# Two decoder layers on one core: the compress of the cached pages moved behind the projection, the first feed-forward's output product in three passes

## The reference

```python
def _layer(x, f_in, f_out, g, b, mixer):
    x = _ln(ALPHA * x + 0.5 * _swiglu(x, f_in[0], f_out[0]), g[0], b[0])
    m, new = mixer(x)
    x = _ln(ALPHA * x + m, g[1], b[1])
    x = _ln(ALPHA * x + 0.5 * _swiglu(x, f_in[1], f_out[1]), g[2], b[2])
    return x, new

def _swiglu(x, w_in, w_out):
    gate, up = jnp.split(x @ w_in, 2, axis=-1)
    return (jax.nn.silu(gate) * up) @ w_out

def _compress(x, pe, w1, w2):
    B, L, K, D = x.shape
    sub = x.reshape(B, L // CMP_STRIDE, CMP_STRIDE, K, D)
    first = jnp.einsum('bnjkd,jde->bnke', sub, w1[:CMP_STRIDE])
    second = jnp.einsum('bnjkd,jde->bnke', sub, w1[CMP_STRIDE:])
    pe_term = jnp.einsum('jd,jde->e', pe, w1)
    hid = jax.nn.gelu(first[:, :-1] + second[:, 1:] + pe_term)
    return jnp.einsum('bnke,ed->bnkd', hid, w2)
```

## Time and profile before

| what | value |
|---|---|
| timed runs, median of 3 | 2906.67 us (2905.1 to 2910.49) |
| the profiled execution | 2892.05 us, its span 2890.5 us |
| TensorE busy / DVE / ACT / POOL | 92% / 36% / 26% / 12% of the span |
| mean granted clock of TensorE | 0.938 |
| bytes moved | 265.81 MB, mean 92 GB/s |
| chain that ended last | PE 49%, issue 37%, DVE 4%, POOL 3%, DMA 2% |

### The profile page before, as it was taken

One profiled execution on the slowest core, in us unless ns is written; L12 is line 12 of the kernel. 1 busy time (PEld: TensorE's weight loads), 2 busy tenths in 40 slices (PEclk: granted clock), 3 DMA queues, 4 the chain that ended last, 5 costly groups with the idle time before them and its releaser, 6 DMA issues.

```text
span 2890.5 us, 49314 instructions
## 1 busy us (share of the span) xinstructions
PE 2668.9 (92%) x17788; PEld 2379.9 (82%) x17788; DVE 1046.9 (36%) x2036; ACT 764.2 (26%) x1167; POOL 342.8 (12%) x321
## 2 busy tenths in 40 slices
PE   7999999997789899999899999999978998999996
PEld 7999788896356889999889997888944567999995
DVE  2222121535555642232432211224456557222415
ACT  2222000422243332231232210013213433222313
POOL 0000000024231200013100000001241311000240
PEclk9999999997699899999999999999955999999998
DMA  3222443114431122222122234321153301222222
GB/s 134 88 87 87 156 137 111 53 61 138 138 86 45 59 69 88 87 88 81 70 88 87 87 105 155 126 91 61 46 179 103 89 30 59 88 87 87 89 80 80
DMA packets 110003, 265.81 MB, mean 92 GB/s; under 512 B 15348, under 2 KB 85139, under 8 KB 90771
## 3 DMA queue, kind: packets, MB, share of 16 engines
q1 hardware_dynamic: 99778, 233.21, 23.9%
q0 software_dynamic: 10080, 30.73, 3.3%
HBM read 258.15 MB, written 14.24 MB: 94 GB/s over the span
## 4 chain that ended last, share of the span: by engine, by line
PE 49%; issue 37%; DVE 4%; POOL 3%; DMA 2%; SPq 2%; DVEq 1%; ACT 1%; POOLq 1%; PEldq 0%; PEld 0%; ACTq 0%
PE PS L458 48%; POOL wo_lo L389 2%; SPq L315 1%; POOL wi_lo L447 1%; DVEq L1424 1%; DMA WO<-wo_dram 1%; POOLq L398 1%; DMA M<-slc_k_dram 1%; DVE xs L1542 0%; DMA WI<-wi_dram 0%; POOLq L402 0%; DVE sm L1888 0%; DVE wi_lo L1427 0%; DVE Z L1719 0%; DVE Z L1427 0%
## 5 line engine op out<-in xcount | busy, mean ns | idle before, releaser
L458 PE MATMUL PS<-xs,wi_hi 128*128 128x272 f32 x5376 | 1018.7, 289 | 20.3 <-DVE wi_lo L1427 18.4
L458 PE MATMUL PS<-xs,wi_lo 128*128 128x272 f32 x3088 | 898.9, 291 | 0.0
L458 PEld LDWEIGHTS PS<-xs,wi_hi 128*128 128x128 f32 x5376 | 849.0, 190 | 21.6 <-issue 21.6
L458 PEld LDWEIGHTS PS<-xs,wi_lo 128*128 128x128 f32 x3088 | 589.7, 191 | 0.0
L389 POOL TENSOR_TENSOR wo_lo<-WO,wo_hi 128x2816 fp32r<-128x2816 f32 x24 | 151.0, 6291 | 1911.6 <-ACT wo_hi L1113 1911.6
L458 PE MATMUL PS<-H,WO 128*128 128x272 f32 x1408 | 332.1, 397 | 6.3 <-DMA WO<-wo_dram 4.8
L1427 DVE TENSOR_TENSOR wi_lo<-WI,wi_hi 128x2048 fp32r<-128x2048 f32 x85 | 194.8, 2292 | 368.7 <-ACT wi_hi L1113 368.7
L458 PEld LDWEIGHTS PS<-H,WO 128*128 128x128 f32 x1408 | 269.0, 192 | 67.3 <-issue 12.0
L458 PE MATMUL PS<-wo_hi,xs 128*128 128x352 f32 x960 | 239.2, 328 | 14.6 <-DVE xs L1542 8.2
L1113 ACT ACTIVATE wi_hi<-WI 128x2048 fp32r<-128x2048 f32 x85 | 162.7, 1914 | 289.1 <-DMA WI<-wi_dram 289.1
L458 PE MATMUL PS<-h_hi,wo_hi 128*128 128x272 f32 x704 | 207.2, 294 | 24.5 <-POOL wo_lo L389 14.1
(11 more groups left out here) (202 smaller groups left out, 3095.4 us busy)
## 6 DMA issues: line engine op xcount, KB each, us to landing
WI<-wi_dram SPq DMA_DIRECT2D x100, 1024.0 KB, 4.8
WO<-wo_dram SPq DMA_DIRECT2D x44, 1408.0 KB, 6.0
M<-cmp_t_dram SPq DMA_DIRECT2D x256, 128.0 KB, 2.2
M<-slc_k_dram SPq DMA_DIRECT2D x128, 64.0 KB, 2.1
M<-slc_k_dram POOLq DMA_DIRECT2D x128, 64.0 KB, 2.5
M<-slc_v_dram SPq DMA_DIRECT2D x128, 64.0 KB, 2.1
M<-slc_v_dram POOLq DMA_DIRECT2D x128, 64.0 KB, 2.3
o_win_s_dram<-win_rows_dram POOLq DMA_DIRECT2D x2, 4064.0 KB, 4.0
```

Source lines behind the costliest of these rows:

```text
L458: return nc.tensor.matmul(out, lhsT, rhs, start=start, stop=stop, skip_group_check=True)
```

## The change

The first feed-forward's output product now runs the same code as the second's (`ffn_out(l, f)`), with `round_h`, `low_h`, `low_wo` and `squares` called for it too. h_hi then takes the regions of the compressed keys, so the whole compress moves behind the projection, into a new `compress(l)` on TensorE, ACT and DVE, where it is interleaved with `rows_to_cols` and the prompt's compressed attention. SP and POOL load 8 of a member's 16 pages each. The half of a hidden sum that lies on partitions 0 to 63 is copied by ACT and added by DVE in one operation. `slc_scores(0)` moves from ahead of the attention to unit 4, and every later piece of the table AT by 4 or more units. The two DRAM copies move from behind the first slc_k pages on POOL's queue to right behind the load of PR at the start of the layer. On DVE the gate weights are masked before the rope, and the gMLP's normalisation stands in member 4's turn of the compress.

```diff
@@ -41,11 +41,11 @@
-AT = dict(keys_1=0, cmp_scores=1, cmp_softmax=2, cmp_weights=4, cmp_turn=5, cmp_columns=6, cmp_outputs=7, cmp_take=8,
...
+AT = dict(keys_0=4, keys_1=8, cmp_scores=1, cmp_softmax=2, cmp_weights=4, cmp_turn=5, cmp_columns=6, cmp_outputs=7, cmp_take=8,
...
-CR_DMAS = 4 * NPG + 1 + 2 * NPG + 2 * NPG
+CR_DMAS = 2 * NPG + 1 + 2 * NPG + 2 * NPG
+CR_LATE = 6 * NPG
+NWS = 2 * KD + NCH - 2
...
@@ -294,16 +306,14 @@
-            def load_pages(l, first, n, src, p, width):
-
-                with sp.Fori(0, n // LOT) as g:
-                    pages = nc.values_load_multi_w_load_instructions(
-                        pt_sb[0:1, ds(first + LOT * g, LOT)], engines=[mybir.EngineType.SP],
-                        min_val=0, max_val=NPHYS - 1)[1]
-                    for j, page in enumerate(pages):
-                        sp.dma_start(CR[:, p, ds((LOT * g + j) * width, width)],
-                                     src[ds(l * NPHYS + page, 1), :, :].rearrange("o p n -> p (o n)")
-                                     ).then_inc(cr_full[p], 16)
+            def load_batch(l, b, p):
+
+                pages = nc.values_load_multi_w_load_instructions(
+                    pt_sb[0:1, ds(b * NPG, LOT)], engines=[mybir.EngineType.SP], min_val=0, max_val=NPHYS - 1)[1]
+                for j, page in enumerate(pages):
+                    sp.dma_start(CR[:, p, j * 256:(j + 1) * 256],
+                                 cmp_t[ds(l * NPHYS + page, 1), :, :].rearrange("o p n -> p (o n)")
+                                 ).then_inc(cr_full[p], 16)
...
@@ -334,19 +344,19 @@
-                with sp.Fori(0, B // 2) as i:
-                    for p in range(2):
-                        b = 2 * i + p
-                        load_wo(l, b, p)
-                        sp.wait_ge(cr_freed, at(l, NCR, b + 1))
-                        own(sp)
-                        load_pages(l, b * NPG, NPG, cmp_t, p, 256)
+                ffn_out(l, 0)
                 with sp.Fori(0, NCH // 2) as i:
                     for p in range(2):
                         load_wo(l, KD + 2 * i + p, p)
 
                 sp.wait_ge(wo_done, at(l, NWO, KD + NCH + 2))
                 own(sp)
+                with sp.Fori(0, B // 2) as i:
+                    for p in range(2):
+                        sp.wait_ge(cr_freed, at(l, NCR, 2 * i + p + 1))
+                        own(sp)
+                        load_batch(l, 2 * i + p, p)
+
                 def load_groups(first, src):
                     with sp.Fori(0, 2) as a:
...
@@ -389,6 +399,26 @@
+            def copies(l):
+
+                lw = lw_of(l)
+                ops = lw(o_pool_s, "o b s n -> (o b) s n")
+                pool.dma_start(ops[:, 0:11, :], lw(hist_rows, "o b s n -> (o b) s n")[:, 4:15, :]).then_inc(stored, 16)
+                ows = lw(o_win_s, "o b s n -> (o b) s n")
+                pool.dma_start(ows[:, 0:508, :], lw(win_rows, "o b s n -> (o b) s n")[:, 4:512, :]).then_inc(stored, 16)
+
+            def load_batch(l, b, p):
+
+                pages = nc.values_load_multi_w_load_instructions(
+                    pt_sb[0:1, ds(b * NPG + LOT, LOT)], engines=[mybir.EngineType.Pool],
+                    min_val=0, max_val=NPHYS - 1)[1]
+                for j, page in enumerate(pages):
+                    pool.dma_start(CR[:, p, (LOT + j) * 256:(LOT + j + 1) * 256],
+                                   cmp_t[ds(l * NPHYS + page, 1), :, :].rearrange("o p n -> p (o n)")
+                                   ).then_inc(cr_late[p], 16)
+
...
             pool.wait_ge(tab_loaded, 16)
             own(pool)
             with pool.Fori(0, DEPTH) as l:
+                lw = lw_of(l)
 
                 pool.wait_ge(x_ready, at(l, NX, 1))
                 own(pool)
                 pool.dma_start(PR[:, :], par[ds(l, 1), :, :].rearrange("o p n -> p (o n)")).then_inc(par_loaded, 16)
+                copies(l)
+                with pool.Fori(0, KD // 2) as i:
+                    for p in range(2):
+                        low_wo(at(l, NWO, p + 1) + 2 * i, p)
                 with pool.Fori(0, NCH // 2 - 1) as i:
                     for p in range(2):
-                        low_wo(at(l, NCH + KD, p + 3) + 2 * i, p)
+                        low_wo(at(l, NWO, KD + p + 3) + 2 * i, p)
                 pool.wait_ge(pj_freed, at(l, 30, 30 + 5))
                 own(pool)
                 pool.wait_ge(wo_done, at(l, NWO, KD + NCH + 2))
                 own(pool)
-                lw = lambda t, n: t[ds(l, 1)].rearrange(n)
                 pool.dma_start(lw(o_pool_p, "o s n -> (o s) n"), pj[P - 15:P, NT - 1, C_P:C_P + 256]).then_inc(stored, 16)
+                with pool.Fori(0, B // 2) as i:
+                    for p in range(2):
+                        pool.wait_ge(cr_freed, at(l, NCR, 2 * i + p + 1))
+                        own(pool)
+                        load_batch(l, 2 * i + p, p)
                 load_groups(l, B, slc_k, 0)
-                ops = lw(o_pool_s, "o b s n -> (o b) s n")
-                pool.dma_start(ops[:, 0:11, :], lw(hist_rows, "o b s n -> (o b) s n")[:, 4:15, :]).then_inc(stored, 16)
                 pool.dma_start(lw(o_pool_s, "o b s n -> (o b) s n")[:, 11:15, :],
                                pj[0:NS, NT, C_P:C_P + 256]).then_inc(stored, 16)
                 ows = lw(o_win_s, "o b s n -> (o b) s n")
-                pool.dma_start(ows[:, 0:508, :], lw(win_rows, "o b s n -> (o b) s n")[:, 4:512, :]).then_inc(stored, 16)
                 pool.wait_ge(rope_ready, at(l, 5, 5))
                 own(pool)
                 for i, (op, os) in enumerate(((o_cmp_p, o_cmp_s), (o_slc_p, o_slc_s), (o_win_p, None))):
@@ -448,7 +484,7 @@
                                             wm_hi[:, n % 2, :, :].bitcast(F32), ALU.subtract).then_inc(wm_split, 1)
...
@@ -511,8 +547,8 @@
-            def ffn_out_3(l, bo):
-                y0 = Y_AT[2]
+            def ffn_out(l, f):
...
-                            pe.wait_ge(h_split, at(l, KF // 2, k // 2 + 1))
+                            pe.wait_ge(h_split, at(l, KF, KF // 2 * f + k // 2 + 1))
...
+
+                def last_item():
+
+                    begin(KD // 2 - 1, 1)
+                    for a in range(2):
+                        for k in range(KF):
+                            last = products(1, k, a)
+                            if (a, k) == (1, 4):
+                                ln_stats(l, 0, 0)
+                        last.then_inc(half_ready, 1)
+                    pe.drain().then_inc(wo_done, 1)
...
@@ -681,72 +683,64 @@
+            def hidden(l, b, v):
+
+                q, p = part(b, v), b % 2
+                if v == 0:
+                    pe.wait_ge(cr_full[p], 16 * at(l, CR_DMAS, LOT * (b // 2 + 1)))
+                    pe.wait_ge(cr_late[p], 16 * at(l, CR_LATE, LOT * (b // 2 + 1)))
+                if q >= 2:
+                    pe.wait_ge(hp_ready, at(l, 18, q - 1))
+                    own(pe)
+                pages = CR[:, p, :].rearrange("p (g c j h n) -> p c j h g n", g=NPG, c=2, j=8, h=2)
+                for j in range(8):
+                    last = mm(PS[:, 6 + v, 0:256], w1[:, 8 * v + j, :], pages[:, v, j, :, :, :], j == 0, j == 7)
+                last.then_inc(cm_ready, 1)
+                if v == 1:
+                    pe.drain().then_inc(cr_freed, 1)
+
...
@@ -891,39 +882,71 @@
+            def prompt_turn(l, t):
+                pe.wait_ge(cp_dve, at(l, 9, max(1, 2 * t)))
+                own(pe)
...
+            def compress(l):
+
+                compress_pe(l)
+                hidden(l, 0, 0)
+                hidden(l, 0, 1)
+                rows_to_cols(l)
+                keys_out(l, 0, 0)
+                keys_out(l, 0, 1)
+                hidden(l, 1, 0)
+                hidden(l, 1, 1)
+                pe.wait_ge(tr_freed, at(l, 10, 10 + 2))
+                own(pe)
+                prompt_hidden(l, 0)
+                prompt_hidden(l, 1)
+                keys_out(l, 1, 0)
+                keys_out(l, 1, 1)
+                hidden(l, 2, 0)
+                hidden(l, 2, 1)
+                prompt_out(l, 0)
+                prompt_out(l, 1)
+                prompt_scores(l)
+                keys_out(l, 2, 0)
+                keys_out(l, 2, 1)
+                hidden(l, 3, 0)
+                hidden(l, 3, 1)
+                keys_out(l, 3, 0)
+                for b in range(4, B):
+                    hidden(l, b, 0)
+                    if b >= 5:
+                        prompt_values(l, b - 5)
                     else:
+                        keys_out(l, b - 1, 1)
+                    hidden(l, b, 1)
+                    keys_out(l, b, 0)
+                    prompt_turn(l, b - 4)
+                    keys_out(l, b, 1)
+                prompt_values(l, NT - 1)
...
@@ -1274,22 +1283,41 @@
+            def hidden(l, q, bank, n):
+
+                v = q % 2
+                act.wait_ge(cm_ready, at(l, 18, q + 1))
```

(15 more changed lines are left out.)

448 lines of the change are left out of this document (190 added, 258 removed).

## The result

| | kernel before | changed kernel |
|---|---|---|
| timed runs, median | 2905.89 us (2899.5 to 2910.49, 4 runs) | 2959.43 us (2947.14 to 2968.64, 4 runs) |
| ratio to before | | 1.0189, 95% interval 1.0162 to 1.0217 |
| profiled execution, span | 2892.05, 2890.5 us | 2960.86, 2959.2 us |
| the same programs once more, on another chip | 2902.87 us (17 runs) | 2943.62 us (6 runs), 1.0133 (1.0102 to 1.0164) |

Slower, as forecast, but by 53.5 us in place of 23, and outside the range by 2. In a second set the same program was 41 us slower. So two sizes have to be explained: what the change costs, and what makes executions of one program differ by 30 us.

What follows compares the result with a forecast made beforehand. TensorE, busy for 92% of the span, was taken as the bound. Per layer 92.4 - 83.7 = +8.7, twice 17.4, plus 5.5: +23, 2915 profiled, 2928 timed; range 2885 to 2957.

Steps and rivals of the forecast that it cites:

- Product in three passes: First feed-forward's output product: chunks every 16.45 us in place of 28.79, gain 83.7 per layer (80 to 88).
- Compress stretch: TensorE between projection and attention, with the compress moved in: ends at 798.2 in place of 719.13, +79.1 us.
- the walk: Step-by-step timing of TensorE from the projection's last copy at 662.4 to 798.2; chance 0.5 for the whole main case.
- rival 1: Between projection and attention: clock stays full, hidden sums 7.07 not 9.3, some 15 us a layer less, 2900; chance 0.22.
- The prompt's hidden sums: 64 instructions between projection and attention: 9.5 us taken, in place of 13.86 in the row before.
- the two ends that I had: Limits for the prompt's hidden sums: 7 us if the clock were full, 13.9 if half.
- My own reading: In the prompt's hidden sums, 217 ns looks like two loads: 13.9 us even at full clock, 4.4 longer per layer.
- Attention paced by POOL's page issues: Attention up to unit 17: waits for slc_k pages of 11.5 and 7.1 us at units 12 and 16; unit 17 +92.4.
- Start of the layer: Copy of 4064 KB beside the load of WI: +5.5 us (0 to 12) in layer 2, 0 in layer 1.
- the bound that I drew from it: At layer 2's start, the WI load shares with the copy, taking up to twice as long: at most 6.5 us.
- Behind unit 17: Rest of the attention after unit 17: the same work is left, so 0 us added.
- The 14.6 us: Timed median 2906.67 lies 14.6 us above the profiled execution of 2892.05; carried over to the changed kernel, 2915 to about 2929.

Runs made afterwards that it cites:

- Fixed pages: Changed kernel with POOL loading its half of the slc_k pages from fixed page numbers, not the page table: 2921.58 us, 1.0075 of the kernel before.

## Why the prediction was right or wrong

**Product in three passes: right.** First product at 309.5, where 306.8 plus the layer's late start of 2.9 is 309.7. POOL's 6.16 and 7.30 hold up h_lo, eleven of which take 23.79; first chunk's end at 331.0 (forecast 327 + 2.9); chunks 16.48 apart; the 3.09 of wo_lo at 438.88 just ahead of the first half's add at 441.89; second part of the projection at 466.4 (463.9 + 2.9). The gain was 83.6 and 80.2.

**Compress stretch: right.** Counted from the last copy, the walk against the trace: hidden(0) starts at 13.6 (12.9 measured), hidden(1) ends at 43.2 (44.0), the prompt's scores at 72.5 (74.3), hidden(3) at 83.3 (85.3), hidden(4) at 94.5 (94.0), unit 0 stands at 135.8 (140.0 in layer 1, 136.1 in layer 2). The 4 us of layer 1 come at its very end, behind member 7; 1.6 of them are the last values' product, 3.60 us where layer 2 has 1.95, at a lower clock (0.77 against 0.98 in the last 11 us of the stretch). Hidden sums took 9.4 to 10.2 up to member 3 and 7.4 later (9.0 for member 5, behind a wait), beside turns and key products, so rival 1 had the warm half right. The prompt's hidden sums took 8.91 (9.5), in part at either clock. Two windows of 2 us in them:

```profile
628.20:630.20 2.00, 2.00 (x20) 2.00 (x19) 0.00 (x0) 0.22 (x1) 0.99 (x2) 1.00 0.20 45
632.20:634.20 2.00, 2.00 (x11) 2.00 (x11) 0.00 (x0) 0.00 (x0) 1.61 (x3) 0.50 0.96 309
```

At clock 1.00 there are 19 to 20 instructions in 2 us, at 0.50 11: some 105 ns and 200. So the two ends that I had, 7 at full clock and 13.9 at half, are both real. The Trainium skill's price of a weight load ("TensorE: Matmul & The Clock Gate", LDWEIGHTS (loading the stationary operand)), 107 ns for 128 columns, agrees at full clock only; at half clock the row is twice that. That it should hold whatever the clock was my addition: the section gives it without naming one. My own reading, that two loads an instruction hold it at 217 at any clock, is refuted.

**Attention paced by POOL's page issues: right.** Waits of 13.2 and 6.1 us at units 12 and 16 (11.5 and 7.1), unit 0 to unit 17 in 68.1 (67.9). Eights of POOL are 9.24 apart. Fixed pages took 18 us off it, and then SP's issues set the pace. Moving the stores let POOL issue sooner, but the last pages then met a load of 2048 KB on the DMA engines, and the wait moved to the next group.

**Start of the layer: the place was right, the price of sharing wrong.** The step that failed is "I take +5.5, from 0 to 12", with "shared in halves the load gets up to twice as long". It got 3.7 times as long. What the DMA engines did in layer 2, issue and landing (count, KB, us to landing), and the busy row of twelve of its microseconds:

```profile
o_win_s_dram<-win_rows_dram POOLq DMA_DIRECT2D x1, 4064.0 KB, 28.5
WI<-wi_dram SPq DMA_DIRECT2D x2, 1024.0 KB, 18.2
```

```profile
1512.00:1524.00 12.00, 12.00 (x85) 12.00 (x84) 0.00 (x0) 0.00 (x0) 0.00 (x0) 0.85 0.38 164
```

The load on the chain took 24.1 us (the row's 18.2 is the middle of two loads, 12.2 and 24.1) beside a copy of 4064 KB that took 28.5, and in these twelve microseconds the engines were busy for 0.38 of the time and moved 164 GB/s. So the load didn't share a full pipe in halves. The queue rows of five microseconds, 1515 to 1520, show what it did share (packets, MB, share of the 16 engines' time; the software queue, q0, is POOL's, q1 is SP's):

```profile
q0 software_dynamic: 15, 0.98, 45.4%
q1 hardware_dynamic: 15, 0.12, 5.8%
```

Packet stands against packet, 15 to 15, but one of the copy is 65 KB and one of the load 8 KB. Taken one by one in the trace, the copy is 64 packets of 65,024 bytes and 2.40 us, eight at a time, and behind each goes one of the load's 8,192 bytes, 0.31 us, so that the next eight start 2.7 later. The load has 128 packets, 8 for each engine if they are spread evenly over the 16; an engine that works on the copy too needs 8 x 2.71 = 21.7 us for its 8 (an estimate from these rows), near the 24.1 measured. The copy keeps only eight engines busy: both shares together are 0.51, and the other half is idle once its part of the load is done. The Trainium skill's rule ("DMA: Bandwidth & Descriptors", Queues, rings and completion order) that engines take turns packet by packet agrees with these rows, but the bound that I drew from it, twice at most, holds only for packets of one size. Not all of the 17.6 came out at the end, as TensorE did 48 more products ahead of that wait, worth 6 us: the net shift is 11.6 in layer 2, and 2.9 in layer 1, where I had counted 0. The experiments with the copies at two other places give it back.

**Behind unit 17: the step "from there the same work is left" failed.** Unit 17 to the attention's end in layer 1, before and after (columns as above):

```profile
773.66:945.50 171.84, 151.35 (x977) 92.58 (x976) 91.20 (x269) 68.57 (x180) 38.86 (x65) 0.92 0.21 62
789.90:978.40 188.50, 172.26 (x976) 105.96 (x976) 91.13 (x268) 69.03 (x179) 38.97 (x65) 0.79 0.23 68
```

The work is the same (977 and 976 TensorE instructions recorded, no wait over 2 us in the changed kernel), the clock isn't: 0.92 and 0.79. It took 16.6 and 10.8 us more than in the one profile of before that I had. I took that profile's attention ends for fixed; they were one end of a draw, and the change's first profile had the other end in both layers. The 14.6 us between that profile and the timed median, which I carried over as a constant, are mostly something else: in the kernel before the clock falls late in 6 of 8 attentions, and the fourth profile, in which both are late too, has a span of 2899.3, 9 us above the first. What makes up those 9 is open. Over four profiles each, unit 17 to the end takes 180.1 us on average in the changed kernel and 173.8 in the kernel before, 12.5 in the two layers together.

**Sum.** By the steps of the first two profiles, with the mean of four behind unit 17: 14.5 - 163.8 + 189.7 + 12.5 = 53; mean spans of four profiles differ by 46, the timed sets by 53 and 41. Of the 30 us by which 53 exceeds the forecast, 9 are the layer starts, 12.5 the attention behind unit 17, and 8.5 small ones in the product and the stretch. Whether the first set's 2959 rather than 2944 was the chip or the hour is open: single executions of the changed kernel lie between 2931 and 2969.
